# Gated delta rule: the next head's preparation placed three pieces a halt within the levels of the inverse

## The reference, cut to what matters

```python
qkv = silu(centred_dwconv(qkv, conv_w))          # five taps
q, k = l2norm(q) * DKA ** -0.5, l2norm(k)
a_strict = tril(k_beta @ k.T * decay, -1);  t_mat = a_strict + I
u = solve(t_mat, v_beta);  w = solve(t_mat, k_beta * exp(gc))
# then a scan over chunks that carries the state
o = rmsnorm(o_forward + o_backward, norm_g) * silu(z)
```

## Time and profile before

| | |
|---|---|
| median of 3 runs | 4129.35 us (4128.23 to 4131.54) |
| the profiled execution | 4124.45 us, its span 4122.7 us |
| granted TensorE clock, mean | 0.919 of full speed |
| busy share of the span | PE 86%, PEld 70%, DVE 55%, ACT 33%, POOL 14% |
| the stage `Gdn` in the span | about 1200 to 1665 us and 2700 to 3170 us |

### The profile page before, as it was taken

One profiled execution on the slowest core, in us unless ns is written; L12 is line 12 of the kernel. 1 busy time (PEld: TensorE's weight loads), 2 busy tenths in 40 slices (PEclk: granted clock), 3 DMA queues, 4 the chain that ended last, 5 costly groups with the idle time before them and its releaser, 6 DMA issues. The chain is left out here.

```text
span 4122.7 us, 48497 instructions
## 1 busy us (share of the span) xinstructions
PE 3533.6 (86%) x17648; PEld 2905.9 (70%) x17648; DVE 2286.6 (55%) x4342; ACT 1380.9 (33%) x2570; POOL 579.9 (14%) x450
## 2 busy tenths in 40 slices
PE   7887888878689999778879999889998779789997
PEld 5666667666567888556757888668887557567886
DVE  3566634656437875567754333348875657663333
ACT  3313333133323333333434332233332334434321
POOL 1000010000103333111111110103333100112110
PEclk9988889888899999899989999999999889889999
DMA  4620036311253222222223333442222212323332
GB/s 127 179 85 28 19 97 171 90 37 31 57 146 105 77 66 62 67 59 78 81 74 105 96 96 92 108 138 72 84 69 80 59 51 61 106 83 91 97 97 72
DMA packets 554066, 350.06 MB, mean 85 GB/s; under 512 B 73412, under 2 KB 497348, under 8 KB 553564
## 3 DMA queue, kind: packets, MB, share of 16 engines
q1 hardware_dynamic: 553820, 346.84, 29.7%
HBM read 301.36 MB, written 45.42 MB: 84 GB/s over the span
## 5 line engine op out<-in xcount | busy, mean ns | idle before, releaser
L556 PE MATMUL bank<-h,w_hi 128*128 128x512 f32 x2240 | 963.0, 430 | 193.6 <-DVE w_low L549 158.6
L557 PE MATMUL bank<-h,w_hi 128*128 128x512 f32 x2240 | 910.2, 406 | 0.0
L558 PE MATMUL bank<-h,w_low 128*128 128x512 f32 x2240 | 908.5, 406 | 0.0
L543 ACT CAST w_hi<-w 128x1024 fp32r<-128x1024 f32 (+2 forms) x456 | 432.5, 950 | 826.2 <-DMA w<-in_w_mlp 395.3
L556 PEld LDWEIGHTS bank<-h,w_hi 128*128 128x128 f32 x2240 | 441.8, 197 | 313.9 <-DVE w_low L549 169.8
L549 DVE TENSOR_TENSOR w_low<-w,w_hi 128x1024 fp32r<-128x1024 f32 (+2 forms) x456 | 528.9, 1161 | 85.2 <-ACT w_hi L543 80.1
L558 PEld LDWEIGHTS bank<-h,w_low 128*128 128x128 f32 x2240 | 439.9, 196 | 102.7
L557 PEld LDWEIGHTS bank<-h,w_hi 128*128 128x128 f32 x2240 | 442.8, 198 | 92.4 <-issue 9.5
L557 PE MATMUL bank<-yT_low,w_hi 128*128 128x512 f32 x768 | 314.3, 409 | 0.0
L1161 ACT ACTIVATE prob<-bank,softmax_stat 128x512 f32<-128x512 f32 (+3 forms) x256 | 145.0, 567 | 293.0 <-DVE softmax_stat L1193 227.2
L556 PE MATMUL bank<-yT_low,w_hi 128*128 128x512 f32 x384 | 166.3, 433 | 56.6 <-DVE xT L685 43.1
(11 more groups left out here) (420 smaller groups left out, 6142.9 us busy)
## 6 DMA issues: line engine op xcount, KB each, us to landing
w<-in_w_in SPq DMA_DIRECT2D x148, 512.0 KB, 4.2
w<-in_w_mlp SPq DMA_DIRECT2D x128, 512.0 KB, 4.0
z<-z_tile SPq DMA_DIRECT2D x164, 256.0 KB, 4.1
w<-in_w_gate SPq DMA_DIRECT2D x64, 512.0 KB, 4.1
q_twice<-z SPq DMA_DIRECT2D x128, 128.0 KB, 2.9
w<-in_w_branch SPq DMA_DIRECT2D x64, 256.0 KB, 2.9
k_twice<-z SPq DMA_DIRECT2D x88, 128.0 KB, 3.7
w<-in_w_out SPq DMA_DIRECT2D x32, 256.0 KB, 2.8
```

Source lines behind the costliest of these rows:

```text
L543: self.a.copy(self.wh[s][:, 0:d, 0:n], self.w[s][:, 0:d, 0:n]).then_inc(self.w_high.sem, 1)
L556: self.t.matmul(bank[0:n, :], wh, high, start=j == 0, stop=False)
L557: self.t.matmul(bank[0:n, :], wh, low, start=False, stop=False)
L558: return self.t.matmul(bank[0:n, :], wl, high, start=False, stop=j == self.depth(i) - 1)
```

## The change

```diff
-    AHEAD = (0, 0, 0) + (2,) * 12 + (2,) + (1,) * 8 + (1, 1)
+    AHEAD = (0, 0, 0) + (3,) * 11 + (1,) + (0,) + (0,) * 8 + (0, 0)
```

## The result

The changed kernel takes 4158.5 us in the median of four runs (4154.42 to 4162.34) against 4128.79 for the kernel before (four runs): a ratio of 1.0071, 95% interval [1.0053, 1.0088]. The forecast was 4162. So timed runs give the loss to some 10 us. For single parts I go by windows of the profiled executions, which repeat better: the two sums shown next are 347.6 and 115.5 us in this execution of the changed kernel and 345.8 and 115.5 in the second, and two other kernels of this document, profiled twice, repeat their levels to 0.6 and 1.4 us. The kernel before was profiled once.

What follows compares the result with a forecast made beforehand. TensorE, busy for 86% of the span, was taken as the bound, with VectorE setting the pace in prepared heads' levels; A 16.8, B 10.8 and C 5 sum to 32.6 us, on 4129.35 giving 4162 us, range 4139 to 4188.

Steps and rivals of the forecast that it cites:

- TensorE's own pieces: z's transposes and two products with ones leave the scan for halts 11 to 13: 1.9 us moved, costed at 0.
- the norm's wait: First layer: TensorE's 12.6 us in four waits at halts 24 and 25, forecast to stay as it was.
- A: Before level five: more VectorE work ahead of the fourth level's subtraction, 4.6 us a head less slack, 16.8 us in all.
- C: Early levels: TensorE's clock drops after added waits, 1.5 us in three of six heads, 5 us in all.
- The slacks: Fourth level, subtraction's end to next level's first product: 1.01, 2.85 or 0.25 us read, other three heads taken by these.
- The wait for the first tanh: Halt 5, pieces 7 to 9: VectorE newly waits for ScalarE's tanh, 0.75 us a head with semaphores.
- the third tanh: Halt 10, pieces 22 to 24: costs VectorE 0.75 us again, taken as hidden at the fifth level.
- level five's slack: Head 1, fifth level: 2.14 us between the subtraction's end and the next level's first product.
- B: Level six, halts 12 and 13: TensorE waits for ScalarE's square in the norms, 1.8 us in six heads, 10.8 us.
- the bare chain: Level six: ScalarE's Ln, table load, Exp, copy and square make TensorE wait 1.3 us before multiplying by ones again.
- the microsecond for the stream's cast: Level six: one weight cast of the stream on ScalarE lengthens TensorE's wait by about a microsecond.

Runs made afterwards that it cites:

- the opposite list: Against the kernel before, fewer pieces in the early halts, 16 in the levels and 18 in the scan: 4118.08 us, ratio 0.9980.

## Why the prediction was right

**The place.** The levels lose, the scan gives nothing back but TensorE's own pieces, and the norm's wait stays: each as forecast. Head 3, forecast at 44.5 us, and halts 15 to 23, forecast at 19.3, are at 45.4 (1623.4 to 1668.9, from the starts of L2620 and L2642) and 19.25 in the mean of six. The levels of heads 0 to 2, forecast at 53 to 57 us, took 57.4 to 58.3, in the second execution 55.1 to 58.3: mostly above the forecast.

**A and C, early levels and clock: 21.8 us forecast.** The time from the first product of level one to that of level five, in six heads, grew by 23.8 us: 13.2 in the first layer, 10.6 in the second (108.4 to 119.0). These are the sums for the first layer's three heads, changed kernel, and then before:

```profile
sum 120.40, PE 102.64 PEld 92.35 DVE 115.57 ACT 21.52 POOL 74.46; mean PE 34.21 PEld 30.78 DVE 38.52 ACT 7.17 POOL 24.82
...
sum 107.20, PE 98.10 PEld 90.27 DVE 101.54 ACT 22.59 POOL 75.05; mean PE 32.70 PEld 30.09 DVE 33.85 ACT 7.53 POOL 25.02
```

VectorE's busy time there grew by 4.7 us a head (4.1 in the second layer), GpSimd's hardly.

The granted clock divides the 23.8. In the windows of the six heads' levels, the share of the clock that was not granted, times the length, adds up to 6.8 us in the kernel before, 13.7 in the changed one and 11.9 in its second execution, all of it ahead of level five in the first two. So C is some 5 to 7 us, an estimate that takes TensorE as busy in all of these stretches, where I had 5; and A is about 17, where I had 16.8. In head 0 of the first layer the second execution had the full clock throughout and took 55.1 us for the levels, the first had 0.94 and took 58.1.

That A's sum is so close is in part luck. The slacks were right: the three heads that I had taken by others have 2.70, 1.01 and 2.84 us in the trace of before, where I had 2.85, 1.01 and 2.85. But one slack, at the fourth level, doesn't decide what a head loses. TensorE waited where level two starts (3.49 us in head 0, 1.91 in head 1) and at level four (1.17, 3.03 and 0.49 in heads 0, 1 and 2), because every level has a subtraction of its own with pieces in front of it. Without the clock's share the six heads lost 3.5, 3.7, 2.6, 1.8, 2.4 and 3.0 us, where I had 1.75, 3.6, 1.75, 4.35, 3.6 and 1.75: the sums agree, most of the heads don't. The wait for the first tanh was sized rightly: 0.7, 0.1 and 1.3 us in three heads against 0.75 each; in head 1 a drain of the stream stood in between.

**A term put at nothing.** I let the third tanh and pieces 22 to 27 fall into level five's slack. That slack of 2.14 us was one of head 1, and it is VectorE's alone; the tanh holds up ScalarE's copies too. With 24 pieces brought forward and no piece in level five, that level still lost 6.4 us in six heads. In the changed kernel the first layer's stage has no such wait of TensorE for the copies, where z's transposes now stand; how much of the 6.4 remains there beside the moved pieces I can't tell.

**B, the norms: 10.8 us forecast,** 9.3 by the windows, 14.7 by the timed runs, whose intervals overlap. The wait itself was 1.2 to 1.5 us a head where I took 1.8; the bare chain had given 1.3, and the microsecond for the stream's cast was not needed, as it fell ahead of the chain.

**The sum.** 32.6 us forecast, 38.3 and 36.5 by the windows, 30 and 41 by two timed comparisons. The direction, the place and the waits were right. That the first timed median, 4158.5, came within 4 us of 4162 is in part luck: the second was 4166.5, and the windows are 4 to 6 us above the sum, by the term that was left out.

What stays open: C is known from the granted clock only, as no run changed the clock and nothing else. And neither the wait for the tanh nor the place of the third tanh was tried alone.

## What to carry to other kernels

Before moving work to another place, look which engine paces each stretch. Head 1's levels, with VectorE busy for 97%, had no room for more of its work. The scan, paced by TensorE, took such work, but not for nothing: it grew by 1.3 us a head under the opposite list. Where two engines slow each other (VectorE and GpSimd here), look at both loads: taking work of either out of head 1's levels shortened them. And denser packing shortens the distance between a piece and the piece of another engine that it waits for. In the changed kernel the first and third tanh of a head share a halt with the piece that waits for them, and VectorE waited 0.7 to 1.3 us in five of six such places in the first layer; the second is a halt away, and it waited in none of three. That a halt in between would cure the others is not shown by a run. And look what else stands behind such a piece in the other engine's queue: here it was the copies that TensorE needed.

## What the runs showed of the hardware

In head 1 of the kernel before, the amount by which VectorE slows beside GpSimd is the whole price of the preparation in the levels: taking 5.6 us of work from GpSimd took 4.2 us from VectorE's busy time in the same 51 instructions and 3.9 us from the levels. In head 2 it is not (49.4 us stay).

After a wait of 3.03 us TensorE's next 16 products took 3.12 us, and after one of 1.91 us (level two of the same head) 2.32, where 16 products with no wait ahead take 1.95:

```profile
1431.24 2.32 PE L2620 MATMUL bank<-M,LT 128*128 128x128 f32 x16 [1.91 <-DVE M L2777]
```

Only the first of these is the clock. The windows of the two, granted clock third from the end:

```profile
1431.20:1433.40 2.20, 2.10 (x17) 1.97 (x17) 2.20 (x4) 0.59 (x1) 0.95 (x1) 1.00 0.00 0
1450.40:1453.40 3.00, 2.93 (x17) 2.77 (x18) 3.00 (x4) 0.59 (x1) 1.27 (x1) 0.72 0.09 25
```

At full clock the products behind a wait took 2.32 or 2.33 us whether the wait was 0.16 us (level three of this head) or 2.05 (head 0 in the second execution). What the 0.37 us are is not shown. And the length of the last wait alone doesn't decide whether the clock falls: it fell with a wait of 1.81 us in the kernel before, where the granted clock of the 3.4 us behind it is 0.55, and not with those of 1.91 and 2.05.
